# Three edits to a fused three-block kernel: carried parts of a scan scaled by ScalarE, one projection half by seven products, residual rows added in PSUM

## Time and profile before

| | us |
|---|---|
| median of 3 runs | 3062.03 (3059.36 to 3065.68) |
| profiled execution, its own time | 3063.29 |
| its span in the trace | 3061.1 |
| PE busy | 2920.9 (95% of the span) |
| DVE busy | 1462.5 (48%) |
| ACT busy | 680.8 (22%) |
| POOL busy | 174.6 (6%) |

### The profile page before, as it was taken

One profiled execution on the slowest core, in us unless ns is written; L12 is line 12 of the kernel. 1 busy time (PEld: TensorE's weight loads), 2 busy tenths in 40 slices (PEclk: granted clock), 3 DMA queues, 4 the chain that ended last, 5 costly groups with the idle time before them and its releaser, 6 DMA issues. The chain is left out here.

```text
span 3061.1 us, 38340 instructions
## 1 busy us (share of the span) xinstructions
PE 2920.9 (95%) x14904; PEld 2113.1 (69%) x14904; DVE 1462.5 (48%) x2644; ACT 680.8 (22%) x1612; POOL 174.6 (6%) x229
## 2 busy tenths in 40 slices
PE   8999999999999899879999999999899998999996
PEld 7678757888868678868788887877776653333332
DVE  6554415333343577586543354425644233444345
ACT  2421113220010464531101101105531221111111
POOL 1000000000000210340100001010000010000000
PEclk9999999999999999999999999998899998999998
DMA  5131212222221112101222232222012138999994
GB/s 178 56 110 55 82 63 83 83 90 83 83 85 57 56 31 98 66 6 65 72 93 83 83 107 86 83 86 83 1 70 74 64 126 368 400 422 425 422 422 199
DMA packets 128455, 397.81 MB, mean 130 GB/s; under 512 B 7875, under 2 KB 36948, under 8 KB 107698
## 3 DMA queue, kind: packets, MB, share of 16 engines
q1 hardware_dynamic: 122586, 382.66, 32.6%
q0 software_dynamic: 3728, 6.76, 0.8%
q10 hardware_dynamic: 1992, 6.33, 0.6%
HBM read 395.93 MB, written 4.20 MB: 131 GB/s over the span
## 5 line engine op out<-in xcount | busy, mean ns | idle before, releaser
L777 PE MATMUL bank<-arena 128*128 128x256 f32 x5488 | 1192.0, 380 | 15.3 <-ACT spare L928 3.4
L777 PEld LDWEIGHTS bank<-arena 128*128 128x128 f32 x5488 | 1041.8, 190 | 162.9 <-issue 12.4
L1089 PE MATMUL bank<-arena 128*128 128x256 f32 x1652 | 366.0, 385 | 9.6 <-PEq L132 3.0
L1089 PEld LDWEIGHTS bank<-arena 128*128 128x128 f32 x1652 | 319.1, 194 | 55.1 <-issue 10.9
L388 PE MATMUL bank<-arena 128*128 128x512 f32 x384 | 166.0, 593 | 4.2 <-PEq L1752 2.0
L4357 DVE TENSOR_TENSOR arena<-arena,bank 128x512 f32<-128x512 f32 x128 | 87.7, 687 | 129.4 <-PE bank L4253 126.6
L841 DVE TENSOR_TENSOR arena<-arena 128x1024 f32<-128x1024 f32 x49 | 60.0, 1225 | 172.4 <-PE bank L777 160.6
L388 PEld LDWEIGHTS bank<-arena 128*128 128x128 f32 x384 | 72.5, 190 | 94.3 <-issue 94.3
L4253 PE MATMUL bank<-arena 128*128 128x512 f32 x256 | 123.1, 616 | 5.1 <-DVE arena L4330 5.1
L1115 DVE TENSOR_TENSOR arena<-arena 128x1024 f32<-128x1024 f32 (+1 forms) x60 | 72.3, 1205 | 98.2 <-PE bank L1089 93.0
L4225 PE MATMUL bank<-arena 128*32 128x512 f32 x1016 | 114.3, 594 | 2.8 <-DMA arena<-in_moe_w_up_dram 2.7
(11 more groups left out here) (628 smaller groups left out, 3417.3 us busy)
## 6 DMA issues: line engine op xcount, KB each, us to landing
arena<-in_moe_w_up_dram SPq DMA_DIRECT2D x64, 1024.0 KB, 15.7
arena<-in_moe_w_down_dram SPq DMA_DIRECT2D x32, 2048.0 KB, 19.8
arena<-in_moe_w_gate_dram SPq DMA_DIRECT2D x63, 1024.0 KB, 13.7
arena<-in_w_in_dram SPq DMA_DIRECT2D x29, 2048.0 KB, 7.9
arena<-in_w_ff_dram SPq DMA_DIRECT2D x16, 2048.0 KB, 7.7
arena<-in_w_out_dram SPq DMA_DIRECT2D x8, 2048.0 KB, 7.9
arena<-in_w_gate_dram SPq DMA_DIRECT2D x11, 1024.0 KB, 5.3
arena<-in_w_up_dram SPq DMA_DIRECT2D x11, 1024.0 KB, 8.0
```

Of the source, the lines that this page charges most:

```text
L777: last = pe.matmul(bank[:, m, :], lhsT, rhs, start=fresh and m == 0 and k == 0, stop=k == 3, skip_group_check=True)
L1089: last = pe.matmul(bank[:, m, :], x[:, k, m * P:(m + 1) * P], w[:, k, :], start=opening and m == 0 and k == 0, stop=k == w.shape[1] - 1, s ...
```

## The change

1. **Scan.** The products with the carried forward and backward state of a step go into one new group "carried" (two products into the two halves of a bank), which ScalarE empties: eight `activation` Copy instructions of 128 x 64 with a scale per partition, into one of two halves of `tmp`, now 1024 wide. VectorE adds both tiles' parts with one `tensor_tensor` of 128 x 2 x 256, in the emptying of the next y group (`add_carried`). ScalarE waits, before it writes a half of `tmp`, for the y group in which VectorE read that half last. `back_group` is gone.
2. **Projection.** It runs by `sevens_and_layer_norm` with one weight piece of eight chunks by 512 columns for each half: the first half by seven products, the second tile by tile with all eight chunks. The sums of the first half are added to x and their statistics taken ahead of the second half's tiles.
3. **End.** TensorE puts x itself into the banks (an identity times the rows, L4340 in the changed kernel), five of the eight before it waits for the last outputs, and the mixes accumulate on them. VectorE reads statistics and mean-subtraction straight from the banks, without an addition. The last tile's last step and its store are cut in two halves.

```diff
@@ -1039,6 +1039,7 @@
+        self.one_half = hidden.shape[1] <= KD
...
@@ -1182,9 +1183,14 @@
 
-        free = ((self.c21_done, 1), (self.first_copied, 2), (self.fifth_copied, 2), (self.joined, 2))
-        left = (((self.joined_three, 2), (self.c11_done, 2)), ((self.c12_done, 2), (self.c21_done, 2)),
-                ((used, 2),), copied(0))
+        if self.one_half:
+            free = (None, (self.c21_done, 1), (self.first_copied, 1), (self.fifth_copied, 1))
+            left = (((self.joined, 1), (self.joined_three, 1)), ((self.c11_done, 1), (self.c12_done, 1)),
+                    ((used, 2),), copied(0))
+        else:
+            free = ((self.c21_done, 1), (self.first_copied, 2), (self.fifth_copied, 2), (self.joined, 2))
+            left = (((self.joined_three, 2), (self.c11_done, 2)), ((self.c12_done, 2), (self.c21_done, 2)),
...
@@ -1236,7 +1244,7 @@
-    sevens = RowSevens(c, name, hidden, (1, 0), (5, 0), ((5, 3072), (5, 3584), (9, 2048), (9, 2560)), made)
+    sevens = RowSevens(c, name, hidden, (1, 0), (5, 0), ((5, 3072), (5, 3584)) + rest, made)
...
@@ -1269,7 +1277,7 @@
                 if n == sevens.per_half - 1:
-                    sevens.dve(dve, 0, n + 1)
...
@@ -1281,11 +1289,17 @@
             for i in range(NT):
-                join(i, 1)
-                dve.wait_ge(filled.sem, filled.at(i + 1))
-                dve.wait_ge(order.sem, order.sent)
-                dve.tensor_tensor(x[:, i, 512:1024], x[:, i, 512:1024], sevens.tile_bank(i)[:, :],
-                                  ALU.add).then_inc(used.sem, used.up())
+                if sevens.one_half:
+                    dve.wait_ge(filled.sem, filled.at(i + 1))
+                    dve.scalar_tensor_tensor(out=x[:, i, 512:1024], in0=x[:, i, 512:1024], scalar=ALPHA,
+                                             in1=sevens.tile_bank(i)[:, :], op0=ALU.mult,
+                                             op1=ALU.add).then_inc(used.sem, used.up())
+                else:
+                    join(i, 1)
+                    dve.wait_ge(filled.sem, filled.at(i + 1))
+                    dve.wait_ge(order.sem, order.sent)
+                    dve.tensor_tensor(x[:, i, 512:1024], x[:, i, 512:1024], sevens.tile_bank(i)[:, :],
+                                      ALU.add).then_inc(used.sem, used.up())
                 dve.wait_ge(used.sem, used.at(i + 1))
...
@@ -2955,35 +2971,53 @@
-            if i:
-                last = pe.matmul(bank[:, 256:512], CT[:, g, i * P:(i + 1) * P], states[0][:, g, :], start=True, stop=True,
-                                 skip_group_check=True)
             return last
...
             if g == 0:
                 dve.wait_ge(skipped.sem, skipped.at(i + 1))
-            if i:
-                dve.tensor_tensor(four(tmp[:, 0, 0:256]), four(bank[:, 256:512]), heads4(grow, 0, i, g, SHD),
-                                  ALU.mult).then_inc(order.sem, order.up())
+            if n > SG:
+                add_carried(dve, n - 1).then_inc(order.sem, order.up())
                 dve.wait_ge(order.sem, order.sent)
-                dve.tensor_tensor(o, o, tmp[:, 0, 0:256], ALU.add).then_inc(order.sem, order.up())
-            dve.wait_ge(order.sem, order.sent)
             return dve.tensor_tensor(o, o, bank[:, 0:256], ALU.add)
-        return ((), prods, (), "v", empty, [at["cb", n]] + ([at["state", i - 1, g]] if i else []))
...
+
+        i, g = n // SG, n % SG
+        lo, hi = min(i, NT - 1 - i), max(i, NT - 1 - i)
+        scaled = c.signals["bank_emptied_by_scalar"]
+        dve.wait_ge(skipped.sem, skipped.at(hi + 1))
+        dve.wait_ge(scaled.sem, scaled.at(by_scalar["carried", n]))
+        o = y[:, lo:hi + 1:hi - lo, g * 256:(g + 1) * 256]
+        return dve.tensor_tensor(o, o, tmp[:, n % 2, :].rearrange("p (t e) -> p t e", t=2), ALU.add)
+
+    def carried_group(n, i, g):
+
+        tiles = ((0, i), (1, NT - 1 - i)) if i < NT - 1 - i else ((1, NT - 1 - i), (0, i))
+
+        def prods(pe, bank):
+            for k, (d, tile) in enumerate(tiles):
+                last = pe.matmul(bank[:, k * 256:(k + 1) * 256], CT[:, g, tile * P:(tile + 1) * P], states[d][:, g, :],
+                                 start=True, stop=True, skip_group_check=True)
+            return last
+
+        def empty(act, bank, order):
+            added = c.signals["bank_emptied_by_vector"]
+            if n - 2 >= SG:
+                act.wait_ge(added.sem, added.at(by_vector["y", (n - 1) // SG, (n - 1) % SG]))
+            for k, (d, tile) in enumerate(tiles):
+                for r in range(4):
+                    h, lo = 4 * g + r, k * 256 + r * SHD
+                    last = act.activation(tmp[:, n % 2, lo:lo + SHD], bank[:, lo:lo + SHD], ACT.Copy,
+                                          scale=grow[:, d, tile, h:h + 1])
+            return last
+        return ((), prods, (), "a", empty, [at["state", i - 1, g], at["right", NT - i, g]])
+
+    def last_carried(dve, order):
+        add_carried(dve, NT * SG - 1).then_inc(order.sem, order.up())
+        dve.wait_ge(order.sem, order.sent)
 
...
@@ -2994,13 +3028,13 @@
+            if i:
+                add_group(("carried", n - 3), carried_group(n - 3, i, g))
             if i < NT - 1:
                 add_group(("state", i, g), update(0, i, g, i == 0, [at["decay", n - 3]]))
-            if i:
-                add_group(("back", j, g), back_group(j, g))
             if j:
                 add_group(("right", j, g), update(1, j, g, i == 0, [at["decay", n - 3]]))
-    bank_groups(c, groups, chained=True, meanwhile=skips_and_factors)
+    bank_groups(c, groups, chained=True, meanwhile=skips_and_factors, after_v=last_carried)
...
@@ -3183,9 +3217,9 @@
-    down_and_layer_norm(c, [("w_out_3", n) for n in (0, 4)], mixT, a["ln1_g_3"][0], a["ln1_b_3"][0],
-                        c.region(9, 0, 2, D), EPS2,
-                        follow=Follower(c, steps, xT, (10, 0), (8, 0), (11, 0)))
+    sevens_and_layer_norm(c, "w_out_3", mixT, a["ln1_g_3"][0], a["ln1_b_3"][0], c.region(9, 0, 2, D),
+                          c.region(7, 0, NT, D), EPS2, Follower(c, steps, xT, (10, 0), (8, 0), (11, 0)),
+                          rest=((8, 3072), (8, 3584)))
...
@@ -4162,10 +4196,11 @@
-            for i in range(NT):
+            for i in range(NT + 1):
                 sync.wait_ge(normed.sem, normed.at(i + 1))
-                sync.dma_start(result[0, i * P:(i + 1) * P, :], x[:, i, :]).then_inc(written.sem, 16)
-            sync.wait_ge(written.sem, written.at(16 * NT))
+                tile, cols = min(i, NT - 1), (slice(0, D) if i < NT - 1 else slice((i - NT + 1) * 512, (i - NT + 2) * 512))
+                sync.dma_start(result[0, tile * P:(tile + 1) * P, cols], x[:, tile, cols]).then_inc(written.sem, 16)
+            sync.wait_ge(written.sem, written.at(16 * (NT + 1)))
...
@@ -4301,12 +4336,24 @@
+            def rows_to_bank(j):
+                pe.matmul(c.banks[j][:, :], c.ident[:, :], x[:, j // 2, (j % 2) * 512:(j % 2 + 1) * 512], start=True,
+                          stop=False)
+
+            pe.wait_ge(added.sem, more * 8 + START)
+            for j in range(5):
+                rows_to_bank(j)
             pe.wait_ge(y_copied_v.sem, more * 2 + 2)
             pe.wait_ge(y_copied_a.sem, more * 2 + 2)
             pe.wait_ge(woven.sem, more * 4 + 3)
-            pe.wait_ge(added.sem, more * 8 + START)
-            for j in range(2 * NT):
-                mix(j, c.banks[j])
+            for i in range(NT):
+                if i == 2:
+                    rows_to_bank(5)
+                elif i == 3:
+                    rows_to_bank(6)
+                    rows_to_bank(7)
+                mix(2 * i, c.banks[2 * i], False)
+                mix(2 * i + 1, c.banks[2 * i + 1], False)
...
@@ -4401,32 +4448,31 @@
-            def normalize(i, last):
+            def normalize(i):
                 dve.wait_ge(order.sem, order.sent)
-                dve.scalar_tensor_tensor(out=x[:, i, :], in0=x[:, i, :], scalar=mv[:, i, 0:1], in1=gain, op0=ALU.subtract,
-                                         op1=ALU.mult).then_inc(gained.sem, gained.up())
+                for half in range(2):
+                    cols = slice(half * 512, (half + 1) * 512)
+                    dve.scalar_tensor_tensor(out=x[:, i, cols], in0=c.banks[2 * i + half][:, :], scalar=mv[:, i, 0:1],
+                                             in1=gain[:, cols], op0=ALU.subtract, op1=ALU.mult).then_inc(gained.sem,
+                                                                                                        gained.up())
                 dve.wait_ge(root.sem, root.at(i + 1))
                 dve.reciprocal(sd[:, i:i + 1], sd[:, i:i + 1]).then_inc(order.sem, order.up())
                 dve.wait_ge(order.sem, order.sent)
-                dve.wait_ge(gained.sem, gained.at(i + 1))
-                dve.scalar_tensor_tensor(out=x[:, i, :], in0=x[:, i, :], scalar=sd[:, i:i + 1], in1=bias, op0=ALU.mult,
```

(25 more changed lines are left out.)

32 lines of the change are left out of this document (13 added, 19 removed).

## The result

| | before, us | changed, us |
|---|---|---|
| median of 5 runs | 3062.03 (3059.36 to 3070.28) | 3035.17 (3035.02 to 3037.17) |
| profiled execution, its span | 3061.1 | 3033.7 |
| PE busy | 2920.9 (95%) | 2918.3 (96%) |
| DVE busy | 1462.5 (48%) | 1460.6 (48%) |
| ACT busy | 680.8 (22%) | 703.2 (23%) |

The ratio is 0.9914, 95% interval 0.9901 to 0.9926: faster by 26.9 us. The forecast was 19.8, with a range down to 3036.0. So sign and places were right, and the gain is 7 us larger than the sum.

What follows compares the result with a forecast made beforehand. VectorE was taken to bound the scan and the end's tiles, TensorE the projection. Terms -9.3 - 3.3 - 7.2 = -19.8 from the 3062.03 us median gave 3042.2 us, range 3036 to 3050.

Steps and rivals of the forecast that it cites:

- Scan: Scan stage: VectorE's work per step falls as ScalarE takes over scaling; -9.3 us, bounds -6 and -11.
- a step becomes 5.16 us: Scan: VectorE loses four instructions (-1.82 us) and gains one (0.72), so a step falls from 6.26 to 5.16 us.
- I let TensorE's 4.90 set two steps: Scan's eight steps: two at TensorE's 4.90 us, six at 5.16, together 40.8 against 48.44: -7.6 us.
- I take 2.1: Scan: ScalarE's group of eight 64-column instructions from PSUM takes 2.1 us.
- the last part: Scan behind the last decay products: TensorE, four ScalarE groups, a last VectorE addition; 13.7 against 15.38 us, -1.7.
- GpSimd's addition, counted as hidden: Scan: the hold-up of VectorE by GpSimd's 1.90 us instruction falls into VectorE's slack; 1.1 us if not.
- The rival of instructions that do not overlap: Scan: ScalarE's instructions don't overlap behind PSUM reads, a group takes 2.94 us, scan +2.6, total 3054; 5%.
- Projection: Third block's projection: first half by seven products, 24.2 us in place of 27.5, sums hidden: -3.3, bounds -1.5 and -3.8.
- End: Kernel's end: first statistics 3.1 us sooner, three tiles -3.6, last store -0.5: -7.2 us, bounds -5.5 and -7.8.
- that rival: End: TensorE's clock has fallen before the rows reach the banks, ten instructions at 0.95 us, total 3047.3; 7%.
- I add some us of run-to-run spread: Whole kernel: the terms' own bounds, 3039.4 to 3049.0, widened to a range of 3036 to 3050.

Runs made afterwards that it cites:

- scaled_twice: The changed kernel with each of ScalarE's scaling instructions in the scan followed by a second of the same size: 3051.62 us, ratio 0.9972.
- rows_behind_waits: The changed kernel with the five row products put behind the waits for the copied outputs: 3048.89 us, ratio 0.9951.

## Why the prediction was right, and where it was wrong

- **Scan, mechanism right, mis-sized.** VectorE set the step before and sets it now; the place and the sign of each piece are as forecast, and the term is -11.5 in place of -9.3, a little outside its own bound of -11. Three sizes were off. "a step becomes 5.16 us": it became 4.96. The four instructions taken out and the one put in are worth what was forecast (1.1 us); the other 0.2 came from instructions that stayed and got shorter. Rows of VectorE before, a step with GpSimd's factors beside it and one without:

```profile
1344.49 0.56 DVE L2910 TENSOR_TENSOR spare<-spare,arena 128x256 f32<-128x256 f32 x1
...
1345.54 1.25 DVE L2855 TENSOR_SCALAR arena<-arena 128x128 f32<-128x128 f32 x4
...
1350.76 0.42 DVE L2910 TENSOR_TENSOR spare<-spare,arena 128x256 f32<-128x256 f32 x1
```

In the changed kernel's step above, the same two take 0.42 and 1.17 us: 0.22 us less. "I let TensorE's 4.90 set two steps": these took 4.73 and 4.64, since the 4.90 ran to the end of the last product and not to the next start. "I take 2.1": the group of eight took 1.75, so the last part took 12.6 us (1351.35 to 1363.94), not 13.7. The eight steps and the last part are each 1.1 us better than forecast. One assumption went the other way: GpSimd's addition, counted as hidden, held one of VectorE's instructions for 1.55 us in place of 0.42, and that step took 5.66 us. VectorE waited for L3013 three times, 1.5 us in all, at the very end only. The rival of instructions that do not overlap is refuted by the rows; its arithmetic was sound. By its formulas a group of 3.4 us makes a step of 3.14 + 3.4 = 6.5 us and leaves the scan with next to no gain, and `scaled_twice` measured 6.45 and 64.1 us against 64.4 before.
- **Projection, right**: 24.25 us against 24.2, term -3.3, no wait for VectorE.
- **End, right**: the first tile -3.0 (3.1 forecast), three tiles 1.06 each (1.19; the subtraction in two halves from the banks takes 1.40 us, where 1.27 went before), the rest, from the last statistics on, -1.3 (0.5). The clock stayed at 1.00 behind 0.85 us of idling, and fell to 0.50 behind 5.00 us in `rows_behind_waits`: both sides of that rival are shown. The rival's 0.95 us for an instruction at the lower level was too much; there the first five follow each other at 0.86.
- **The step that failed** is the last one, "I add some us of run-to-run spread". The sum was set against one execution and the median of the kernel before, with no term for TensorE's granted clock in stages whose work does not change, and a lower end only 3.4 us under the one that its terms gave, 3039.4. The runs showed that term to be worth up to 10.8 us between two executions of the changed kernel, and the five of the first measurement, all quick, lie 0.8 us below the range of 3036 to 3050. Of the 7.0 us by which the forecast was missed, 2.4 are the terms (2.2 of them the scan's), the other 4.6 this one. The sum with the terms as measured (-22.2) from 3062.0 is 3039.8; the two later measurements of the change, 3040.3 and 3042.7, lie about it and within 2 us of the forecast of 3042.2, and the five executions of the first all fell among the quick ones (3034.9 to 3037.6 here; the longer ones 3041.6 to 3045.7). Over all 16 executions 9 are quick and 7 long, and the median is 3037.4, 23.7 under the median of the 60 executions of the kernel before, 3061.1.

So of the 26.9 us first measured, some 22 are the change's and some 5 the luck of five executions. Both later measurements, made on two different chips, hold both kinds, so the chip does not decide it. What stays open is what decides, in a given execution, whether a stretch at half clock falls on a place; why the kernel before shows no such second kind below its median (its lowest of 60 executions is 3058.2); and why the five executions of the first measurement agree so well. Shifting a stage on purpose by added work was not tried.

## What to carry to other kernels

When an edit relieves the engine that sets a step, read its remaining instructions back to back: it can still set the step when another engine is busy 99% of the time. Add up all the work of the engine that takes the work over, for each kind of step by itself: here ScalarE was full in five steps and had 2 us to spare in the others, and an average hides that. A gain summed over places in one trace should be checked in place, in two traces, with the same instruction before and behind each edit; medians of a few executions can carry several us that belong to no edit. Put products that need nothing from a wait ahead of it: they spare the idling and the half clock behind it.

## What the runs showed of the hardware, unexpected

- One program, two executions 10.8 us apart: TensorE's clock is granted differently behind the same 2.00 us without matmuls (1.00 against 0.83 over 10 us), and in the branch attention (0.95 against 0.79 over 25 us). The places cost 0.7 to 4.0 us each.
- ScalarE's 64-column instructions from PSUM last 326 ns each (median) but follow each other at 0.20 us, in place of 0.24 from SBUF (2.02 for eight). The Trainium skill, ScalarE: Activation LUTs, section "What ACT_TABLE_LOAD costs", has an ACTIVATE with one pointer operand at 280 ns + 0.833 ns per column, an estimate of 333 ns here, and an overlap of about 93 ns between instructions one behind the other, an estimated pitch of 0.24 us. The trace agrees on the length of one and on the pitch from SBUF; from PSUM the overlap is 130 ns. The pitch is what a chain of them costs.
- Two VectorE multiplications of 256 columns out of PSUM took 0.75 us one behind the other, against 0.42 for each alone.
- VectorE's two instructions of 512 columns took 1.77 us partly beside GpSimd's addition and 1.41 without it; in the scan, one of 256 columns took 1.55 us beside GpSimd's addition of 128x1024, against 0.42.
